# A diffusion trunk layer on one core: 64-token expert steps in two column tiles and four streams, two-head attention, a scan in eight sets, and loads moved ahead

## What is computed

```python
mod = silu(c) @ w_ada + b_ada                       # 6 vectors of 1024, for latents and for context
h = rmsnorm(x, g_pre_mix) * (1 + sc1) + sh1
pa, pq, pk, pv, pc = split(h @ w_in)                # 512, 512, 512, 512, 256 columns
ya = chunk_mlp(pa)                                  # gelu, LayerNorm of one half, 128 x 128 spatial gating
yb = attention(pq, pk, pv)                          # 8 heads of 64; latents: a window of 8 x 16 and the cached context
yc, h_last = s5(pc)                                 # 16 groups, 64 complex states, forward and backward scan
x = x + g1 * rmsnorm(concat(ya, yb, yc) @ w_out, g_post_mix)
h = rmsnorm(x, g_pre_ffn) * (1 + sc2) + sh2
idx, wts = top8_of_64(sigmoid(h @ w_router))        # by groups: 4 of 8
for e in range(64):                                 # tokens that chose expert e
    acc[toks] += (silu(h[toks] @ w_gate[e]) * (h[toks] @ w_up[e])) @ w_down[e] * wts
x = x + g2 * rmsnorm(acc + shared_expert(h), g_post_ffn)
```

## Time and profile before

| what | us |
|---|---|
| runs | 1684.27, 1698.43, 1719.99 |
| span of the profiled execution | 1715.0 |
| its PE busy time | 1522.2 (89%) |
| its DVE, ACT and POOL busy time | 552.6, 303.9, 249.7 |
| its weight loads on PE (PEld, beside PE) | 821.9 |
| its mean granted clock of PE | 0.908 of full speed |

### The profile page before, as it was taken

How to read it: one execution, slowest core, us unless ns; L and a number is a source line. 1 busy time by engine, 2 the same in 40 slices (tenths; PEclk the granted TensorE clock), 3 DMA queues, 4 the chain that set the end, 5 groups by cost and what they waited for, 6 DMA issues and landing times. The chain is left out here.

```text
span 1715.0 us, 18898 instructions
## 1 busy us (share of the span) xinstructions
PE 1522.2 (89%) x5181; PEld 821.9 (48%) x5182; DVE 552.6 (32%) x1639; ACT 303.9 (18%) x637; POOL 249.7 (15%) x262
## 2 busy tenths in 40 slices
PE   5689999989978897999999999999999999998990
PEld 1134653768856454444444444444444444444440
DVE  0037374155543133522222222222222222222223
ACT  0131010132311222111111111111111111111112
POOL 1011000011100000011221221121112212121121
PEclk9799899955658998999999999999999999999995
DMA  9561147091011615188999899999996989879844
GB/s 300 162 226 57 49 163 261 17 258 45 1 70 50 244 45 208 63 333 255 339 325 313 266 333 301 331 317 305 310 307 203 329 248 352 238 230 318 257 101 147
DMA packets 101551, 372.09 MB, mean 217 GB/s; under 512 B 24813, under 2 KB 30076, under 8 KB 75272
## 3 DMA queue, kind: packets, MB, share of 16 engines
q1 hardware_dynamic: 63480, 278.88, 43.7%
q0 software_dynamic: 24944, 86.99, 21.5%
q10 hardware_dynamic: 13088, 5.72, 1.2%
HBM read 313.66 MB, written 57.89 MB: 217 GB/s over the span
## 5 line engine op out<-in xcount | busy, mean ns | idle before, releaser
L1835 PE MATMUL bank<-rings,hT 128*128 x1168 | 514.6, 594 | 1.1 <-DVE hT L1773 1.1
L1835 PEld LDWEIGHTS bank<-rings,hT 128*128 128x128 f32 x1168 | 222.5, 191 | 281.0 <-issue 281.0
L1857 PE MATMUL bank<-downs,w_rt 128*128 x584 | 281.8, 627 | 0.0
L1685 POOL DMA_INDIRECT h<-h2D,toks x76 | 74.2, 976 | 661.4 <-DVE toks L1766 649.6
L1857 PEld LDWEIGHTS bank<-downs,w_rt 128*128 128x128 f32 x584 | 110.2, 199 | 112.8 <-issue 112.8
L1794 DVE COPY w_rt<-bank 128x256 f32<-128x256 f32 x73 | 31.0, 424 | 358.8 <-PE bank L1847 358.8
L1717 ACT ACTIVATE hT<-bank 128x512 f32<-128x512 f32 x75 | 44.8, 597 | 536.2 <-PE bank L1824 535.8
L1704 POOL DMA_INDIRECT accD<-mixedT,dest x73 | 117.1, 1605 | 151.3 <-ACT mixedT L1732 139.9
L1824 PE MATMUL bank<-ident,h 128*128 128x128 f32 x600 | 86.3, 289 | 58.1 <-DMA h<-h2D,toks 56.8
L1732 ACT ACTIVATE mixedT<-bank,gain 128x512 f32<-128x512 f32 x146 | 92.3, 683 | 240.2 <-PE bank L1857 233.0
L1824 PEld LDWEIGHTS bank<-ident,h 128*128 128x128 f32 x600 | 74.1, 193 | 67.3 <-DMA h<-h2D,toks 65.2
(11 more groups left out here) (418 smaller groups left out, 1511.8 us busy)
## 6 DMA issues: line engine op xcount, KB each, us to landing
rings<-w_e_gate SPq DMA_DIRECT2D x64, 1024.0 KB
rings<-w_e_up SPq DMA_DIRECT2D x64, 1024.0 KB
downs<-w_e_down SPq DMA_DIRECT2D x64, 1024.0 KB, 8.4
rings<-w_ada SPq DMA_DIRECT2D x12, 2048.0 KB, 12.4
rings<-w_in SPq DMA_DIRECT2D x4, 2048.0 KB, 9.5
rings<-matD SPq DMA_DIRECT2D x3, 2048.0 KB, 12.8
matD<-rings SPq DMA_DIRECT2D x2, 2048.0 KB, 7.1
rings<-w_out SPq DMA_DIRECT2D x2, 2048.0 KB, 10.8
```

The source lines that it names most:

```text
L1685: pool.indirect_dma_start(out=xg[par], out_offset=None, in_=k.h2D, in_offset=bass.IndirectOffsetOnAxis(ap=toks[par][:, 0:1], axis=0)).then ...
L1835: last = pe.matmul(bank[par][:, :].rearrange("p (x f) -> p x f", x=2), lhsT=xT[par][:, kk * P:(kk + 1) * P], rhs=gu[:, kk], start=(kk == 0 ...
L1857: last = pe.matmul(bank[4 + h][:, :], lhsT=hidT[par][:, kk, :], rhs=down[:, kk, h * 512:(h + 1) * 512], start=(kk == 0), stop=(kk == 1))
```

## The change

All six stages are rewritten at once.

- `project`: x is loaded first and normalised by its root mean square alone. An adaLN chunk is multiplied with 32-column left sides, whose results stand in four column tiles, two products in each. Chunks 0 to 3 are turned into columns and applied to the turned x by DVE; so pa waits for four chunks instead of eight. Chunks 4 to 11 are summed by one product each (`mod`) between the other products. The S5 loads go from ACT's queue to SP's, behind the first w_in chunk, and ssm_b is loaded in long rows and turned on PE. The gating, its LayerNorm, the window mask and the value windows are made here. Three ring slots follow a table `loads`.
- `attend`: twenty units of two heads. Scores of the two heads have 64 rows each in two row tiles, values 64 columns each in two column tiles; the operations on ACT and DVE take both heads.
- `scan`: eight sets of four groups; the inputs of set m + 2 stand between the outputs of earlier sets, and each set has its own scan.
- `route`: the context rows of the second adaLN set are loaded ahead into down buffers; h goes to memory in half rows of 2 KB; experts are sorted by their number of 64-token blocks and dealt into four streams, each stream with its own weight buffer.
- `experts`: a round takes one block of 64 tokens from each of the four streams. Half rows are gathered (two for a token). Gate and up write the two halves of their columns into two 64-column tiles. A stream's next expert is loaded, if the table names one, after its last gate and up. Each output half row is stored in its own place in yD (no adding), with a bounds check that leaves padding out.
- `combine`: it loads all eight outputs of a token (21 MB) and adds them, one half of the columns on DVE and the other by identity products on PE.

The core of the diff:

```diff
-        def ada(c):
-            w = weights()
-            out = begin()
-            for kk in range(KD):
-                pe.matmul(out[0:33, :], lhsT=cS[:, kk, :], rhs=w[:, kk, :], start=(kk == 0), stop=False)
-            end(pe.matmul(out[0:33, :], lhsT=sel[:, c, :], rhs=b12[:, :], start=False, stop=True))
+        def ada(c):
+            w = weights("ada", c)
+            out = begin("ada", c)
+            for r in range(2):
+                for q in range(4):
+                    last = pe.matmul(out[32 * q:32 * q + 32, :], lhsT=cS[:, 2 * q + r, :], rhs=w[:, 2 * q + r, :],
+                                     start=(r == 0), stop=(r == 1))
+            end(last)
...
+    loads = [(("ada", 0), 0), (("ada", 1), 1), (("ada", 2), 2), (("ada", 3), 0), (("in", 0), 1), (("ada", 4), 0),
...
+    jobs += [("pa", 0), ("pa", 1), ("ada", 4), ("pa", 2), ("mod", 4), ("pa", 3), ("ada", 5), ("pa", 4), ("mod", 5)]
...
-            vals = [k.vctx[:, pair]] if t is None else [Vw[:, t, 0, pair], Vw[:, t, 1, pair], cvs[:, pair]]
+            vals = [k.vctx] if t is None else [Vw[:, t, 0, :], Vw[:, t, 1, :], cvs]
...
+                for x, lane in enumerate(lanes):
+                    last = pe.matmul(bank[6 + u % 2][lane, 0:P], lhsT=val[:, (2 * hp + x) * HD:(2 * hp + x + 1) * HD],
+                                     rhs=pT[u % 2][:, x, n * P:(n + 1) * P], start=(n == 0), stop=(n == len(vals) - 1))
...
+        inputs(2)
+        outputs(0)
+        inputs(3)
+        outputs(1)
...
+            ins = sp.dma_start(dst, w[bass.ds(e, 1)].rearrange("o (p k) n -> p (o k n)", k=KD), cond=e > 0)
...
             for kk in range(KD):
-                last = pe.matmul(bank[par][:, :].rearrange("p (x f) -> p x f", x=2), lhsT=xT[par][:, kk * P:(kk + 1) * P],
-                                 rhs=gu[:, kk], start=(kk == 0), stop=(kk == KD - 1))
+                lhsT = xT[par][:, (kk % 4) * P + (kk // 4) * SB:(kk % 4) * P + (kk // 4 + 1) * SB]
+                for h in range(2):
+                    last = pe.matmul(bank[par][h * SB:(h + 1) * SB, 0:F].rearrange("p (x f) -> p x f", x=2), lhsT=lhsT,
+                                     rhs=w[:, kk, :, h * FH:(h + 1) * FH],
+                                     start=(kk == 0), stop=(kk == KD - 1))
...
-                                    in_=yo[u % 2], in_offset=None, compute_op=ALU.add).then_inc(added, 16)
+                                    in_=yo[u], in_offset=None, bounds_check=2 * TOPK * TOK - 1,
+                                    oob_is_err=False).then_inc(added[u], 16)
...
+            for kk in range(2):
+                for h in range(2):
+                    last = pe.matmul(bank[4 + par][h * SB:(h + 1) * SB, :], lhsT=hidT[par][:, kk, :],
+                                     rhs=down[:, kk * D + h * 512:kk * D + (h + 1) * 512], start=(kk == 0), stop=(kk == 1))
...
+                sp.dma_start(stage[t % NS_][:, half], rows[t * P:(t + 1) * P, half]).then_inc(parts_in[t][j], 16)
...
+            parts = stage[t % NS_].rearrange("p (j n) -> p n j", j=TOPK)[:, 0:512, :]
+            dve.tensor_reduce(sums[t % 2][:, :], parts, axis=AX.X, op=ALU.add).then_inc(summed, 1)
```

More of the change, by code:

```diff
@@ L209, in _ @@
+        store(0)
+        load("ada", 11)
         sp.wait_ge(K_taken, 1)
@@ L613, in _, with mod @@
+        def mod(c):
+            pe.wait_ge(acc_taken, at[("ada", c)] + 1)
+            end(pe.matmul(begin("mod", c)[0:2, :], lhsT=sel4[:, :], rhs=pt[c % 2][:, :], start=True, stop=True))
         pe.wait_ge(k.consts, 1)
         pe.wait_ge(cs_ready, 2)
-        pe.wait_ge(small_in, 16)
         ada(0)
+        for t in range(NT):
+            pe.wait_ge(xn_ready, t + 1)
+            for h in range(2):
+                out = begin("xT", (t, h))
+                for kk in range(4):
+                    last = pe.transpose(out[:, kk * P:(kk + 1) * P], X[:, t, 4 * h + kk:D:KD], ident[:, :])
+                end(last)
@@ L628, in turn @@
[L628 to L647 removed]
+        turned_sum(1)
@@ L707, in _ @@
             end(last)
-        done()
+        w = weights("in", 1)
+        columns("q", w, [0])
+        ada(6)
+        columns("q", w, [1])
+        mod(6)
+        ada(7)
+        columns("q", w, [2])
+        mod(7)
+        s5_turned(0)
+        ada(8)
+        s5_turned(1)
+        columns("q", w, [3])
+        mod(8)
+        s5_turned(2)
+        ada(9)
+        s5_turned(3)
+        w = weights("in", 2)
+        columns("k", w, [0], [0])
+        s5_kernels(0)
+        s5_kernels(4)
+        columns("k", w, [0], [1])
+        s5_kernels(8)
+        mod(9)
+        ada(10)
+        s5_kernels(12)
+        columns("k", w, [1])
+        mod(10)
+        ada(11)
+        columns("k", w, [2])
+        mod(11)
+        columns("k", w, [3])
+        out = begin("kctx", 0)
+        pe.wait_ge(acc_taken, at[("k", (3, 1))] + 1)
+        for j in range(4):
+            last = pe.transpose(out[:, j * P:(j + 1) * P], k.kT[:, j, LAT:TOK], ident[:, :])
+        end(last)
+        for h in range(NH_A):
+            last = pe.transpose(bank[7][:, h * P:(h + 1) * P], k.wsp[:, h, :], ident[:, :])
+        last.then_inc(wsp_t, 1)
+        w = weights("in", 3)
+        for t in range(NT):
+            out = begin("v", t)
+            for kk in range(KD):
+                last = pe.matmul(out[:, :], lhsT=hT[:, kk, t * P:(t + 1) * P], rhs=w[:, kk, :],
+                                 start=(kk == 0), stop=(kk == KD - 1))
+            end(last)
+        w = weights("in", 4)
+        for s2 in range(4):
+            channels(w, s2)
+        pe.wait_ge(wsp_taken, 1)
+        pe.wait_ge(vn_ready, 1)
+        pe.wait_ge(K_taken, 1)
+        for h in range(NH_A):
+            pe.matmul(bank[3 + h][:, 0:NT * HD], lhsT=wspT[:, h, :], rhs=k.z[:, :, D_A + h * HD:D_A + (h + 1) * HD],
+                      start=True, stop=True).then_inc(gate_ready, 1)
     scope.close()
@@ L916, in _, with gated @@
+        def gated(n):
+            if n < 2:
+                for t in range(4):
+                    last = pe.transpose(bank[n][:, t * P:(t + 1) * P], k.z[:, t, n * P:(n + 1) * P], ident[:, :])
+            else:
+                for c in range(2):
+                    last = pe.transpose(bank[0][:, c * P:(c + 1) * P], k.z[:, CTX_T, c * P:(c + 1) * P], ident[:, :])
+            last.then_inc(ya_t, 1)
+        scores(0)
+        scores(1)
         pe.wait_ge(cache_in, 32)
@@ L1114, in _, with channels @@
     def _(pe):
[L1115 removed]
+        def channels(n):
+            z, g0, m = halves[n]
             if n >= 2:
@@ L1545, in _, with order, table @@
-        up(NT - 1)
+        def order():
+            pe.wait_ge(sort_ready, 1)
+            pe.matmul(bank[3][:, 0:NE], lhsT=visits_b[:, :], rhs=sort[:, :], start=True, stop=True)
+            pe.matmul(bank[3][:, NE:2 * NE], lhsT=expert_b[:, :], rhs=sort[:, :], start=True, stop=True).then_inc(sorted_ready, 1)
+        def table():
+            pe.wait_ge(word_ready, 1)
+            for u in range(U):
+                last = pe.transpose(bank[3][0:1, u * P:(u + 1) * P], word[:, u:u + 1], ident[:, :])
+            last.then_inc(table_t, 1)
@@ L1627, in _, with first, every_round @@
+    def first(it):
+        return isinstance(it, int) and it == 0
+    def every_round(eng, body):
+        middle = rounds(eng)
+        for u in range(U):
+            body(0, u)
+        with eng.Fori(1, middle + 1) as it:
+            for u in range(U):
+                body(it, u)
+        for u in range(U):
+            body(middle + 1, u, True)
+        return middle + 2
     @block.sync
     def _(sp):
+        sp.wait_ge(k.shared_up, NT)
+        load_gu(sp, k, a, 3, 3)
+        sp.wait_ge(k.shared_down, NT)
+        load_down(sp, k, a, 3, 3)
@@ L1793, in body @@
             dve.wait_ge(hid_t, i + 1)
[L1794 to L1802 removed]
+            dve.tensor_copy(hidT[par], bank[7][:, 0:P].rearrange("p (k n) -> p k n", k=2)).then_inc(hidT_ready, 1)
```

1734 lines of the change are left out of this document (898 added, 836 removed).

## The result

The kernel after takes 1362.02 us (median of four runs, 1359.38 to 1362.47), the kernel before 1708.28 beside it (a fourth run, 1718.13, has joined the three of 1684 to 1720): a ratio of 0.805, 95% interval [0.799, 0.811]. Forecast were 1408 us and 1330 to 1540. The span of the profiled execution is 1360.3 us.

A forecast was written before the change was run, and what follows sets the result against it. PE was taken to bound the expert stage, with DMA close behind. Projection 264 + attention 78 + scan 78 + route 162 + experts 768 + combine 71 = 1421 us, less 1% 1408; range 1330 to 1540.

The forecast's parts named there:

- The expert step: Experts: a 64-token step takes 6.2 us on PE with two tiles side by side, 719 us for 116 steps.
- rival (a): Experts: 64-column tiles no faster than in turn, or clock falls; step 11.35 or about 12 us, about 2000 us; chance 0.05.
- rival (d): Experts: tiling mode changes drain PE, +35 us there and some 5 elsewhere, 1448 us in all; chance 0.09.
- The stalls and margins of the stage: Experts: 25 us of stalls (12 to 60), 10 for first gathers and weights, 14 for last scatters.
- rival (b): Experts and combine: DMA binds, stalls of 60 instead of 25 and 15 to 45 us in the combine, 1473; chance 0.21.
- Attention: Attention stage: two-head units of 4.15 us, 16 of them 66 us, plus some 12: 78 us, −59.
- rival (c): Stages ahead of routing give less (row tiles in series, ada, scan at 100, S5 chain): +60 us, 1468; chance 0.15.
- with both in series 98: Attention: upper end of 98 us if scores and values of two heads do not run side by side.
- Scan: Scan stage: eight sets in a pipeline give 78 us, between 52 and 100, −19.
- Projection: Projection: first pa at 42.5, then 222 us of PE, end 264, −75; two tiles at a time +14, none +62.
- Combine: Combine: 21 MB loaded at 386 GB/s in 54 us, 2 to start, some 15 at the end: 71 us, +46.
- less 1%: Whole kernel: the 1421 us sum lowered by 1%, as the runs' median lay 17 us below the profiled span: 1408.

The follow-up runs named there:

- Experiment 1: The kernel after with a step's gate and up products issued one half after the other instead of alternating: 1671.65 us.
- Experiment 7: The kernel after with scatters adding again into two accumulators in memory, the combine loading two sums instead of eight outputs: 1360.48 us.
- experiment 4: The kernel after with the two heads of an attention unit kept apart in PE's queue: 1408.77 us, its base 1362.38.
- experiment 3: The kernel after with PE's scan order undone, for each direction all four sets' inputs and then all outputs: 1367.04 us.
- experiment 5: The kernel after with every one of the 116 expert steps loading its stream's next weights whether the expert changes or not: 1612.69 us.
- sums2: The kernel of Experiment 7 with the second accumulator starting at zero and DVE alone adding in the combine, POOL idle: 1353.42 us.

## Why the prediction was right, step by step

**The bound and its place** were read rightly: PE set the expert stage, and what PE no longer does came off the time. The DMA did not take its place (0.81 of the engines, 2.7 us of waits).

**The expert step** was put at 6.2 and is 6.18, so the weightiest number, 719 of 1421 us, held, though it stood on two rows of 82 columns that started together. Experiment 1 shows part of rival (a)'s price: with the halves of gate and up one after the other a step is 8.81, 2.63 more where the rival had 3.43 for them; down stayed side by side, so its 11.35 was not measured. The kernel then took 1672 us, still under the kernel before, though a step of 8.7 was to be the point from which it is slower: the rest of the sum was too high.

**Mode changes**, rival (d): by the rates of the earlier trace rows a step's parts need 3.43 + 0.12 + 0.45 + 0.24 + 1.72 = 5.96 us, and it takes 6.18. If all of the difference came from the two changes, they would cost 0.11 us each, 26 us in all; 35 was the upper end, and the sum's 6.2 had already room for it. The rule of the Trainium skill (TensorEngine Tiling (Array Packing), Key Properties) that a change of mode drains the engine is not refuted by that; what it can cost here is bounded by the same 0.11 us.

**The stalls and margins of the stage** are the term that was mis-sized most: "stalls of 12 to 60; I take 25", with 10 and 14 for start and drain, 49 together. The stage took 733.7 us and its 116 steps of 6.18 need 717, so 17 are left: one wait for weights of 2.7 and 1.7 more in the slower products after it, 6.1 from the end of PE's last product (1281.6) to the combine's first load, and some 6 at the start and end of the pipeline. The range rested on 231 GB/s for half rows, a rate of the earlier trace rows that the adding scatter had made; without adding it is 371. Three rounds with eight changes then need 62 + 12 = 74 us of DMA, about what PE takes. Experiment 7 puts the adding back, at 229 GB/s, and 20.4 us of stalls return. So the mechanism of rival (b) exists, but in this kernel the DMA stays just short of it.

**Attention** was put at 78 and took 65.5. The step that failed is "one head's unit at 1.2 GHz ... two heads together 4.15": the durations were carried over at the low clock, and rival (c) too took the low clocks as given. The clock rose at 289 us instead of 461.7, and at 2.4 GHz the unit is 2.86 us, below even the 3.2 of the forecast's lower end; DVE holds it (busy for 9.76 of the 10 us from 300 to 310). Why it rose so early is not shown; experiment 4 shows that it rises later with the heads kept apart, and that it does rise. One sum was wrong as well: in "with both in series 98" only the scores are doubled. With the values too it is 16 x (1.98 + 1.40 + 2.82 + 0.35) + 12 = 117.

**Scan**: 60.7 instead of 78. The forecast's 78 lay between 52 (PE's work at full clock) and 100; the clock was 0.97. Of its reason, a pipeline of eight sets, the order on PE is not what did it (experiment 3); the sets themselves were not tested. Part of the 60.7 is luck: the same code took 67.0 us at a clock of 0.85 in the run of experiment 1.

**Projection** 267.4 for 264: the first pa product at 41.36 for 42.5, waiting for w_in as said. A chunk takes 1.85 us (26.52 to 28.37) for 1.72. In the kernel before it took 6.98, from 20.98 to its bias product at 27.96, so four 32-column tiles ran at 6.98/1.85 = 3.8 times the rate of one. The Trainium skill (TensorE: Matmul & The Clock Gate, Part 3) gives 3.07 times for four row tiles; carried over to these four column tiles that is the forecast's estimate of 2.3 us a chunk, and the trace does not agree. The prices beside the sum were uneven: +14 for two tiles at a time counts eight chunks, +62 for none twelve. No experiment took the projection apart; its 72 us are read from these rows alone.

**Combine** 72.6 for 71, bound by its loads as said, with DVE level beside them, which was not said.

**The last step, "less 1%"**, scaled the sum to the median of the runs. It brought it nearer by luck: the median of the kernel after lies not 1% below its profiled span but 0.1% above it. The four runs of the kernel before lie between 1684 and 1720 (those beside the experiments between 1676 and 1738), the twelve of the kernel after between 1359 and 1368; one profile cannot tell why.

## What to carry to other kernels

When two half-width products are put side by side, write them alternately in the queue and look at their start times: the order of one loop was worth some 300 us here. Work out whether a freed resource was priced by an operation that the change removes (a scatter that adds), for such rates do not carry over; nor need the clock of an old stage hold in the new one. When a change pushes cost to the end (here 48 us of combine), look for slack in the stage that won: with the DMA at 0.81 there, the adding scatter cost the experts some 17 us once their changes were spread, and the combine gave 44 back. And compare kernels stage by stage: a clock that varies in a stage which the edit does not touch was worth up to 8 us here, as much as some of the edits.

## What was not expected of the hardware

- PE at 99% busy was granted 0.56 in the old attention. In experiment 4 it was granted 0.50 for 52 us in which it hardly idled, and then 0.99 with the same instructions in the same order. In the new attention it is busy for 79% at 0.90.
- The clock of the scan was 0.97 in some profiles and 0.81 to 0.85 in others, also where the code up to there was the same (60.7 us in the kernel after, 67.0 in experiment 1).
- PE runs a later tile's instructions beside an earlier tile's although others stand between them, a few instructions deep: four of sixteen in experiment 1, all of the scores and four of six values in experiment 2.
- A DVE operation of 128 x 1024 took 3.18 us beside POOL's subtractions and 1.28 without.
- After some waits for weights of 2 to 4 us gate and up took 5.0 to 6.6 us instead of 3.67: PE came back at the lower clock, so such a stall costs more than its length. In the kernel after this followed its one wait of 2.7 us, in experiment 5 some 35 of its 102 waits, the longest 2.8; after 3.18 us in sums2 it did not.
